# Where the remainders of a three-part bf16 split are kept, and when half of one expert's down weights is loaded

## The reference

```python
def reference(x, ...):
    h = rmsnorm(x, norm_mix_g)
    x = x + hybrid_mixer(h, ...)                  # attention + gated linear attention, then @ w_out
    h = rmsnorm(x, norm_ffn_g)
    x = x + hierarchical_moe(h, ...)              # router, then 32 experts
    return rmsnorm(x, final_norm_g)

def hierarchical_moe(h, ...):
    ...                                           # top-1 group of 4, then top-2 of its 8 experts
    for e in range(N_EXPERTS):
        hid = silu(x @ w_gate[e]) * (x @ w_up[e])
        y = y + combine[:, e:e + 1] * (hid @ w_down[e])
```

## Time and profile before

| | |
|---|---|
| runs | 780.07, 778.24, 777.99 us; median 778.24 |
| profiled execution, its own time | 778.23 us |
| its span in the trace | 776.4 us |
| PE busy | 749.3 us (97%) |
| DVE, ACT, POOL busy | 231.5, 147.0, 93.8 us |
| moved by the DMA engines | 238.84 MB, mean 308 GB/s |

### The profile page before, as it was taken

How to read it: one execution, slowest core, us unless ns; L and a number is a source line. 1 busy time by engine, 2 the same in 40 slices (tenths; PEclk the granted TensorE clock), 3 DMA queues, 4 the chain that set the end, 5 groups by cost and what they waited for, 6 DMA issues and landing times.

```text
span 776.4 us, 13770 instructions
## 1 busy us (share of the span) xinstructions
PE 749.3 (97%) x6184; PEld 373.8 (48%) x6184; DVE 231.5 (30%) x471; ACT 147.0 (19%) x318; POOL 93.8 (12%) x88
## 2 busy tenths in 40 slices
PE   7999999999999999999999999999999999989995
PEld 3444454464455466545464454544645445436431
DVE  2185782005575357211111111121111111111204
ACT  1634230033345442000000000000000000000024
POOL 0681440000000120000100101000010100100002
PEclk9999999999999999999999999999999999999998
DMA  9733230410540669999999999999999999999983
GB/s 318 242 108 108 109 110 6 158 63 0 233 201 1 267 274 366 381 426 424 422 425 425 423 422 429 426 422 422 425 424 425 423 420 421 420 421 420 412 347 133
DMA packets 38510, 238.84 MB, mean 308 GB/s; under 512 B 5958, under 2 KB 7366, under 8 KB 20784
## 3 DMA queue, kind: packets, MB, share of 16 engines
q1 hardware_dynamic: 35968, 233.85, 73.8%
q0 software_dynamic: 2480, 4.06, 1.4%
HBM read 229.65 MB, written 12.32 MB: 312 GB/s over the span
## 4 chain that ended last, share of the span: by engine, by line
PE 82%; DMA 10%; SPq 6%; DVE 1%; ACT 1%; issue 0%; DVEq 0%
PE bank L854 20%; PE bank L505 18%; PE bank L877 11%; DMA arena<-in_w_up 9%; PE bank L817 9%; PE bank L554 4%; PE bank L700 4%; PE bank L744 4%; SPq L445 3%; SPq L446 1%; PE bank L661 1%; PE bank L733 1%; PE bank L866 1%; PE bank L912 1%; PE bank L718 1%; SPq L403 1%
## 5 line engine op out<-in xcount | busy, mean ns | idle before, releaser
L854 PE MATMUL bank<-arena 128*64 128x512 f32 x928 | 205.2, 593 | 8.2 <-DMA arena<-in_w_up 7.4
L505 PE MATMUL bank<-arena 128*128 128x512 f32 x320 | 139.3, 594 | 0.0
L854 PEld LDWEIGHTS bank<-arena 128*64 128x64 f32 x928 | 67.5, 137 | 140.8 <-issue 133.4
L877 PE MATMUL bank<-arena 128*64 128x512 f32 x512 | 116.9, 599 | 0.0
L817 PEld LDWEIGHTS bank<-arena 128*128 128x128 bf16 x3072 | 96.2, 98 | 23.6 <-issue 23.1
L817 PE MATMUL bank<-arena 128*128 128x64 bf16 x3072 | 100.6, 193 | 0.0
L505 PEld LDWEIGHTS bank<-arena 128*128 128x128 f32 x320 | 60.3, 190 | 74.0 <-issue 73.9
L1175 ACT ACTIVATE arena<-bank,arena 128x256 f32<-128x256 f32 x32 | 15.2, 474 | 356.2 <-PE bank L854 313.2
L1710 POOL DMA_INDIRECT y_tok<-arena x31 | 30.3, 978 | 415.0 <-DVE arena L1563 386.7
L1556 DVE SCALAR_TENSOR_TENSOR arena<-bank,arena 128x256 f32<-128x256 f32 x32 | 15.5, 484 | 210.6 <-ACT arena L1175 210.5
L877 PEld LDWEIGHTS bank<-arena 128*64 128x64 f32 x512 | 33.9, 136 | 56.8 <-issue 54.8
(11 more groups left out here) (178 smaller groups left out, 526.1 us busy)
## 6 DMA issues: line engine op xcount, KB each, us to landing
arena<-in_w_down SPq DMA_DIRECT2D x30, 2048.0 KB, 28.3
arena<-in_w_gate SPq DMA_DIRECT2D x24, 2048.0 KB, 26.8
arena<-in_w_up SPq DMA_DIRECT2D x24, 2048.0 KB, 25.5
arena<-in_w_up SPq DMA_DIRECT2D x14, 1024.0 KB, 28.5
arena<-in_w_gate SPq DMA_DIRECT2D x12, 1024.0 KB, 28.4
arena<-in_w_in SPq DMA_DIRECT2D x5, 2048.0 KB, 7.8
arena<-in_w_gate SPq DMA_DIRECT2D x8, 512.0 KB, 14.4
arena<-in_w_down SPq DMA_DIRECT2D x4, 1024.0 KB, 12.4
```

Of the source, the lines that this page charges most:

```text
L505: m = pe.matmul(pbank[unit_bank(n)][:], lhs(k), rhs(k), start=(k == 0), stop=(k == KC - 1))
L854: mm = pe.matmul(both, xT[:, k], gate_and_up(e, k, cols), start=(k == 0), stop=(k == KC - 1))
L877: mm = pe.matmul(pbank[5 + e % RING][64 * half:64 * half + 64, :], hidT[:, kc % 2, kc // 2], down_unit(e)[:, kc, half * 512:(half + 1) * 512],
```

## The change

1. `rest2` is gone. The remainder of tiles 0, 1 and 2 is written over the residual tile itself (`rest_of(t)` is `x1_by_chunk(t)`), that of tile 3 into `last_rest` at 204.5 KiB. So `rest(t, half)` for `t < 3` must now wait until the square sum and the transposes have read the tile, and it stands after `x1_T_evict(t)` in DVE's order. Both `mid` of a tile follow on ACT.
2. The first half of `down_unit(2)` (128 to 136 KiB, where `rest2` lay), 1 MiB, is loaded by `load_half_d(2, 0)` ahead of the loads over the residual. The second half stays where the whole load was, behind `lg_done`.

```diff
@@ -74,9 +74,9 @@
     return 2 + n - GV_UNITS[0] if n in GV_UNITS else n % UNIT_BANKS
 
 
-def landed(e, of_halved, of_3):
-
-    return sum(of_halved if n in HALVED else of_3 if n == 3 else 16 for n in range(e % SETS, e + 1, SETS))
+def landed(e, of_halved, of_3, of_2=16):
+
+    return sum(of_halved if n in HALVED else of_3 if n == 3 else of_2 if n == 2 else 16 for n in range(e % SETS, e + 1, SETS))
 
 
 def ff_chunk(k):
@@ -142,7 +142,7 @@
         scan_keep = at(140, T)
         probs = [at(134 + 2 * i, 2, NKEY) for i in range(4)]
         hT2 = [at(136 + 4 * i, KC, P) for i in range(2)]
-        rest2 = [at(128 + 4 * i, KC, P) for i in range(2)]
+        last_rest = at(204.5, KC, P)
         lr = at(142, T)
         probsT = [at(142, 4, P), at(195, 4, P)]
         x1 = at(144, TT, D)
@@ -341,6 +341,9 @@
         def x1_by_chunk(t):
             return x1[:, t].rearrange("p (k q) -> p k q", k=KC)
 
+        def rest_of(t):
+            return x1_by_chunk(t) if t < TT - 1 else last_rest
+
         halves = [slice(0, KC // 2), slice(KC // 2, KC)]
         all_k = slice(0, KC)
 
@@ -402,6 +405,9 @@
             def load_d(e):
                 sp.dma_start(down_unit(e).rearrange("p (h c) d -> p h (c d)", h=2), wd_d[e]).then_inc(wd_in[e % SETS], 16)
 
+            def load_half_d(e, h):
+                sp.dma_start(flat(down_unit(e)[:, 2 * h:2 * h + 2]), wd_d[e][:, h]).then_inc(wd_in[e % SETS], 16)
+
             sp.wait_ge(unit_done, 25)
             load_g(0)
             load_u(0)
@@ -423,6 +429,7 @@
                 sp.wait_ge(sumsq_done, TT + 2 * (t + 1))
                 sp.dma_start(gate_unit(3)[:, ks], wg_d[3][:, ks]).then_inc(wg_in[3], 16)
 
+            load_half_d(2, 0)
             load_over_residual(0)
             load_over_residual(1)
             sp.wait_ge(wo_done, 2 * TT)
@@ -431,10 +438,10 @@
             load_over_residual(2)
             load_over_residual(3)
             sp.wait_ge(lg_done, TT)
-            load_d(2)
+            load_half_d(2, 1)
             for h in range(2):
                 sp.wait_ge(gu_done if h else gu_half_done, 1)
-                sp.dma_start(down_unit(3)[:, 2 * h:2 * h + 2].rearrange("p c d -> p (c d)"), wd_d[3][:, h]).then_inc(wd_in[3], 16)
+                load_half_d(3, h)
             for e in range(4, LAST):
                 sp.wait_ge(gu_done, e - 3)
                 if e not in HALVED:
@@ -869,7 +876,7 @@
             def down(e):
                 pe.wait_ge(ht_evicted, e + 1)
                 if e < LAST:
-                    pe.wait_ge(wd_in[e % SETS], landed(e, 16, 32))
+                    pe.wait_ge(wd_in[e % SETS], landed(e, 16, 32, 32))
                 for kc in range(FC):
                     if e == LAST and kc % 2 == 0:
                         pe.wait_ge(last_d_in[kc // 2], 16)
@@ -1128,34 +1135,34 @@
 
             def mid(t, half):
                 act.wait_ge(rest_done, 2 * t + half + 1)
-                nc.scalar.copy(h2_part[t][1][:, halves[half]], rest2[t % 2][:, halves[half]]).then_inc(mid_done, 1)
+                nc.scalar.copy(h2_part[t][1][:, halves[half]], rest_of(t)[:, halves[half]]).then_inc(mid_done, 1)
 
             hi(0, 0)
             square(0, 0)
-            mid(0, 0)
             hi(0, 1)
             square(0, 1)
-            mid(0, 1)
             square_root(0)
             hi(1, 0)
             square(1, 0)
-            mid(1, 0)
             hi(1, 1)
             x1_T_evict(0)
             square(1, 1)
-            mid(1, 1)
             square_root(1)
+            mid(0, 0)
+            mid(0, 1)
             hi(2, 0)
             square(2, 0)
-            mid(2, 0)
             x1_T_evict(1)
+            mid(1, 0)
+            mid(1, 1)
             hi(2, 1)
             square(2, 1)
-            mid(2, 1)
             square_root(2)
             x1_T_evict(2)
             hi(3, 0)
             square(3, 0)
+            mid(2, 0)
+            mid(2, 1)
             mid(3, 0)
             hi(3, 1)
             square(3, 1)
@@ -1461,34 +1468,35 @@
 
             def rest(t, half):
                 dve.wait_ge(hi_done, 2 * t + half + 1)
-                if t >= 2:
-                    dve.wait_ge(parts_done, 2 * (t - 2) + half + 1)
-                tt(rest2[t % 2][:, halves[half]], x1_by_chunk(t)[:, halves[half]], h2_part[t][0][:, halves[half]],
+                if t < TT - 1:
+                    dve.wait_ge(sumsq_done, TT + 2 * t + half + 1)
+                    dve.wait_ge(h2T_done, t + 1)
+                tt(rest_of(t)[:, halves[half]], x1_by_chunk(t)[:, halves[half]], h2_part[t][0][:, halves[half]],
                    ALU.subtract).then_inc(rest_done, 1)
 
             residual(0, 0)
-            rest(0, 0)
             residual(0, 1)
-            rest(0, 1)
             residual(1, 0)
             mean_square(0)
-            rest(1, 0)
             inverse_root(0)
             residual(1, 1)
             x1_T_evict(0)
-            rest(1, 1)
+            rest(0, 0)
+            rest(0, 1)
             mean_square(1)
             residual(2, 0)
-            rest(2, 0)
             inverse_root(1)
             x1_T_evict(1)
+            rest(1, 0)
+            rest(1, 1)
             residual(2, 1)
-            rest(2, 1)
             route_groups(0, 2)
             mean_square(2)
             route_experts(0, 2)
             residual(3, 0)
             x1_T_evict(2)
+            rest(2, 0)
+            rest(2, 1)
             rest(3, 0)
             inverse_root(2)
             residual(3, 1)
@@ -1700,7 +1708,7 @@
             for t in range(TT):
                 for half in range(2):
                     pool.wait_ge(mid_done, 2 * t + half + 1)
-                    nc.gpsimd.tensor_tensor(h2_part[t][2][:, halves[half]], rest2[t % 2][:, halves[half]],
+                    nc.gpsimd.tensor_tensor(h2_part[t][2][:, halves[half]], rest_of(t)[:, halves[half]],
                                             h2_part[t][1][:, halves[half]], ALU.subtract).then_inc(parts_done, 1)
 
             last_row = EXPERTS * SLOTS - 1
```

## The result

In ten executions each, the changed kernel takes 780.64 us in the median (779.47 to 782.54), the kernel before 778.78 (777.99 to 780.2). The ratio is 1.0022 with a 95% interval of 1.0011 to 1.0032: slower by 1.7 us by this ratio, by 1.9 between the medians. The profiled execution took 781.25 us, its span is 779.4. In later runs of the same two kernels the ratio was 1.0011 (0.9995 to 1.0027) and 1.0024 (1.0012 to 1.0037).

The account below looks back on a forecast made before the run. The prediction took the queue of weight loads, after its last hole, to set the end. From 778.23 us, a 1.4 us DVE hold-up less 1.2 us from the early load gave +0.2, so 778.4 us, range 776.5 to 780.0.

Parts of the forecast that it names:

- What bounds the kernel: At the end, PE arrives with each load; the load queue's last hole and the bytes after it set the end.
- The early half load: Moving 1 MiB into the queue's hole at 285 to 292 us gains 1.2 us, of 2.47 at most.
- the sign of an error: Expert 4's down weights landing more than 8.5 us after issue would refute the forecast; 7.7 was expected.
- The remainders of tiles 0 and 1: Their later DVE, ACT and POOL operations between the stages cost nothing, since nobody waits for them until the first gather.
- The hold-up of DVE by POOL: Three POOL subtractions at 290.54 to 294.0 block DVE's one-hot and rest(3, 1), delaying the experts by 1.4 us.
- strict turn-taking: DVE's one-hot gets in after POOL's second subtraction, rest(3, 1) after the third, ending at 294.9: 1.4 us late.
- both ways: DVE waiting out all three POOL subtractions, or alternating with them; rest(3, 1) ends at 294.9 either way.
- The clock: Rival: PE's longer wait drops the clock to 1.2 GHz for one pass, +7.1 us, 785.5; 0.11 with other long delays.
- The sum: Experts start 1.4 us late, less 1.2 us in hand in the load queue: 0.2 us later, 778.4 us.
- The base: Starting time for the forecast: the profiled execution of the kernel before, 778.23 us, taken as the median but for 0.01.
- the range: The 8 in 10 interval for the changed kernel's time: 776.5 to 780.0 us.

Follow-up runs that it names:

- load_kept: Kernel before with one remainder buffer, the early half load and two unused products filling PE's wait; ratio 0.9982, median 777.84 us over both runs.
- before_kept: Kernel before with two unused products ahead of the last router product; ratio 1.0006, median 778.96 us over this run and its repeat.
- load_alone: Kernel before with its own orders, one remainder buffer at 204.5 KiB for all tiles, and the early half load; 778.74 us, ratio 0.9992.
- load_kept2: Repeat of load_kept against the kernel before; ratio 0.9984 (0.9968 to 1.0000).
- late_load: Changed kernel with both halves of expert 2's down weights loaded behind the last router product; 781.54 us, ratio to the kernel before 1.0030.
- tile2_early: Changed kernel with tile 2's remainders in the 204.5 KiB buffer and its rest and mid in their old places; 778.30 us, ratio to before 0.9990.
- before_again: Kernel before, unchanged, run against itself; 780.15 us, ratio 1.0006.
- after_kept: Changed kernel with four unused products ahead of the last router product, filling PE's wait; 778.62 us, ratio to the kernel before 0.9988.
- after_again: Changed kernel, unmodified, run again beside late_load2 and against the kernel before; ratio 1.0011.
- after_third: Changed kernel, unmodified, run once more against the kernel before; 780.73 us, ratio 1.0024.
- late_load2: Repeat of late_load, beside the changed kernel on the same chip; 781.83 us, ratio to the kernel before 1.0037.
- pool_late: Kernel before with one POOL wait changed, so that three subtractions follow in a row; 780.97 us, ratio 1.0024.
- wait_alone: Kernel before with two unused ACT copies that lengthen PE's wait ahead of the last router product; 781.76 us, ratio 1.0029.

## Why the prediction was wrong

**What bounds the kernel** held: the end follows the last transfers, 730.79 against 727.78, and PE waits for them 7.2 us in all, about as before (7.4).

**The early half load** was costed at 1.2 us. load_kept against before_kept, the pair that differs in the load, gives 777.84 against 778.96, 1.1 us, and the traces 0.7 to 1.3 us from the first pass to the end. The size is right, but the reading that it came from isn't: expert 4's down weights should have landed 1.2 us sooner after their issue, and with the load in and the experts at 302 they landed after 8.7, 8.7 and 8.6 us (load_alone, load_kept, load_kept2), against 8.9 before. The changed kernel itself showed 7.7 once and 8.8 twice, and over 8.5 was to be the sign of an error. So the 1.2 us are in part luck. That nothing can be gained once the queue has run dry is neither shown nor refuted by late_load.

**The remainders of tiles 0 and 1** at nothing: right as far as tile2_early can tell, whose first pass starts at 302.20.

**The hold-up of DVE by POOL** was right in mechanism and too large: "1.4 us late" was 0.79. The case that happened is the strict turn-taking: POOL's run began at 290.23, so that two subtractions of 1.16 us end at about 292.55, within the one-hot's 292.21 to 292.69; the one-hot got in behind the second, `rest` behind the third. I had both ways at 294.9; it was 294.27, because POOL's run began at 290.23 and not at 290.54 (ACT's first of three casts started at 289.55, directly behind the square sum, where I had left it at the 289.85 of the earlier trace rows), because the one-hot in its midst lengthened it by under 0.1 us and not by 0.2, and because `rest`, issued at 292.73, needed only 0.54 us more when POOL let go at 293.73, not 0.69.

**The clock** is the step that failed. The sum had nothing for it. I wrote "nothing in the trace shows the clock falling on so short a wait", gave the case, together with all else that could delay the start by over 2 us, 0.11, and priced it at 7.1 us, one whole pass at half clock. But one trace is one execution. In the kernel before, too, the clock falls in some executions and not in others: 74 of 123 were under 0.996, and before_again shows the fall behind 0.59 us of wait. The longer wait raises the odds: 33 of 34 executions of the changed kernel were under 0.996, 20 of them in the lowest class, against 25 of 123. Nor is the price a whole pass: the low stretch lasted 3.4 or 6.8 us in each profile and cost 1.5 or 3.0 us of PE's time. With the wait filled, and all else as in the changed kernel, the ratio fell from 1.0022 to 0.9988 (after_kept). What decides in a single execution whether the clock falls wasn't tested.

The sum can be made again with this. Before's own class means with the changed kernel's shares give (1 x 778.7 + 13 x 779.4 + 20 x 780.9) / 34 = 780.3; before's own mean is 779.4. So by this estimate some 0.8 us of the 1.2 by which the two kernels' means differ in all executions comes from the odds alone (in the first result the means differ by 1.8). What is left, 0.4 us, is the hold-up less the load; from 0.8 less 1.1 one would expect -0.3, and the classes are too coarse to settle the rest. The order of the remainders by itself (late_load) costs 2.3 us in the mean. The changed kernel is 1.1 us below that, which the load may or may not account for.

**The base** was off too. I summed against the profiled execution's 778.23 and noted that it is the median of the runs shown, three of them. Of ten the median is 778.78, of the 123 beside the experiments 779.27: the profiled one was among the executions with no fall. That alone moved the forecast by 0.5 to 1.0 us, and the range with it: from 778.78 the same range would have ended at 780.55, just under the measured 780.64. So a part of the miss is the base's; the forecast of the difference, +0.2 us where 1.7 to 1.9 was measured, failed by the clock.

## What to carry to other kernels

If PE waits between dense stretches, even for the half microsecond of this kernel, its time can be a mixture over executions with and without a fallen clock; look at the mean clock of many executions before explaining one trace, and try filling the wait with products nobody reads (a gain of 0.0034 in the ratio with a wait of 1.44 us, none that could be told with 0.59). Don't bunch GpSimd operations into a stretch in which VectorE does two-operand work on the critical path, even if neither engine is short of time. To free a buffer for an earlier load, look first for another free corner of the memory (here 4 KiB at 204.5) before moving operations: together with the filler it gave 0.9982 and 0.9984.

## What the runs showed of the hardware

- Between the stages the granted clock fell to 0.50 for 3.4 us behind a wait of PE of 0.59 us (before_again), 1.44 (after_again), 1.45 (after_third, late_load2) and 1.64 (pool_late), and for 6.8 us behind one of 1.44 (the first profile of the changed kernel) and 1.42 (wait_alone). It held with 1.44 us in late_load, and with 0.60 and 0.59 in the first profile, load_alone and tile2_early. At 714 and 719 us it fell for 3.4 us behind waits of 2.87 and 2.88 us (tile2_early, wait_alone). The fall came 0.8 to 2.7 us after the wait had ended, and the two of 6.8 us are those that came soonest, after 0.8 and 1.0 us. Each time the clock came back to 1.00 while PE worked on.
- DVE got in between two POOL subtractions that each wait on a semaphore: the one-hot ended at 292.69, 0.14 us behind the second of them. It had not between the 24 additions of the earlier trace rows. The Trainium skill (SBUF — State Buffer, "SBUF: two separate sides") has the lock held for a whole instruction; the trace agrees, with the one-hot's 0.48 and `rest`'s 1.54 us, and adds that a run of three isn't one lock. I didn't try what makes the difference.
- `rest`, held up by POOL's last subtraction, finished 0.54 us after that ended (293.73 to 294.27), where it takes 0.69 us from its issue.
